# Five large weight matrices of a hybrid decoder block laid out as contiguous 128-column tiles in device memory

## The reference

```python
mod = silu(c) @ w_ada + b_ada            # shift1, scale1, gate1, shift2, scale2, gate2
h    = rmsnorm(x, norm1_g) * (1 + scale1) + shift1
proj = h @ w_in                          # 4096 x 19520: NSA q | NSA k,v | gates(48) | FoX q,k,v | f(16) | merge gates
o_nsa = nsa(...);  o_fox = fox(...)      # two attention mixers, 2048 wide each
g = sigmoid(merge gates)
y = g[..., :D] * (o_nsa @ w_up_nsa) + g[..., D:] * (o_fox @ w_up_fox)
x = x + gate1 * (y @ w_out)              # 4096 x 4096
h2 = rmsnorm(x, norm2_g) * (1 + scale2) + shift2
x = x + gate2 * (square(relu(h2 @ w_ff1)) @ w_ff2)   # 4096 x 16384, 16384 x 4096
```

## Time and profile before

| what | value |
| --- | --- |
| timed runs | 12343.16, 12598.13 (median), 12849.61 us |
| span of the profiled execution, slowest core (5) | 12165.9 us |
| spans of the eight cores | 11995.2 to 12165.9 us |
| PE busy | 9543.8 us, 78% of the span |
| DMA of POOL's queue | 759.01 MB, 66.0% of 16 engines |
| DMA of SP's queue | 329.89 MB, 10.5% of 16 engines |
| chain that ended last | PE 66%, DMA 18%, DVE 6%, ACT 4% |

### The profile page before, as it was taken

How to read it: one execution, slowest core, us unless ns; L and a number is a source line. 1 busy time by engine, 2 the same in 40 slices (tenths; PEclk the granted TensorE clock), 3 DMA queues, 4 the chain that set the end, 5 groups by cost and what they waited for, 6 DMA issues and landing times.

```text
span 12165.9 us, 128077 instructions; the slowest of 8 cores (11995.2 to 12165.9 us)
## 1 busy us (share of the span) xinstructions
PE 9543.8 (78%) x49482; PEld 4455.4 (37%) x49482; DVE 1449.5 (12%) x3744; ACT 1785.7 (15%) x3025; POOL 1166.2 (10%) x830
## 2 busy tenths in 40 slices
PE   1188967888999966666668987598789879987988
PEld 1133332333444434332223433244334334433443
DVE  0101022110000011222322100200000001000000
ACT  0111121112100035322221000200000000000000
POOL 1010000000111100000002300010001001100100
PEclk9887878899999977655557999799889989998999
DMA  9785645677888879533336997799889879988997
GB/s 144 138 90 64 69 92 65 70 71 78 83 93 95 96 123 147 86 56 63 46 60 76 107 108 115 88 68 108 100 75 82 111 93 74 98 106 83 77 107 104
DMA packets 2909954, 1097.08 MB, mean 90 GB/s; under 512 B 2315184, under 2 KB 2897200, under 8 KB 2906288
## 3 DMA queue, kind: packets, MB, share of 16 engines
q0 software_dynamic: 2392608, 759.01, 66.0%
q1 hardware_dynamic: 516752, 329.89, 10.5%
HBM read 1709.32 MB, written 138.41 MB: 152 GB/s over the span
## 4 chain that ended last, share of the span: by engine, by line
PE 66%; DMA 18%; DVE 6%; ACT 4%; issue 4%; SPq 1%; DVEq 0%; another core or an unknown queue 0%; ACTq 0%; POOL 0%; POOLq 0%
PE ps L237 64%; DMA xq_257<-out 5%; DMA ws_55<-w_ada 4%; DMA xq_256<-out 4%; PE ps L240 2%; SPq L266 1%; DMA xp_239<-xc 1%; DVE xr_258 L246 1%; DMA xp_238<-xc 1%; DMA fv_159<-d_fv 1%; DMA ws_56<-w_ff 1%; DVEq L128 0%; ACT hT L243 0%; DVE oaccS L256 0%
## 5 line engine op out<-in xcount | busy, mean ns | idle before, releaser
L237 PE MATMUL ps<-hT,ws_56 128*128 128x512 bf16 x2752 | 643.7, 398 | 18.4 <-DMA ws_56<-w_in 18.0
L237 PE MATMUL ps<-hT,ws_53 128*128 128x512 bf16 (+1 forms) x2688 | 620.0, 394 | 19.2 <-DMA ws_53<-w_in 18.1
L237 PE MATMUL ps<-hT,ws_55 128*128 128x512 bf16 x2688 | 620.4, 394 | 0.6
L237 PE MATMUL ps<-hT,ws_52 128*128 128x512 bf16 (+1 forms) x2688 | 616.1, 392 | 1.5 <-DVE yb_129 L256 0.5
L237 PE MATMUL ps<-hT,ws_54 128*128 128x512 bf16 x2688 | 616.4, 392 | 0.9
L240 PE MATMUL ps<-cf,tn_255 128*128 128x128 f32 x1024 | 180.1, 305 | 501.3 <-DVE xr_258 L246 465.6
L243 ACT ACTIVATE tn_255<-ps,modT 128x512 f32<-128x512 f32 x256 | 175.9, 687 | 2349.1 <-PE ps L240 2315.9
L237 PE MATMUL ps<-oT,ws_56 128*128 128x512 bf16 x2080 | 461.7, 383 | 44.9 <-DMA ws_56<-w_ff 44.9
L237 PE MATMUL ps<-oT,ws_55 128*128 128x512 bf16 x2080 | 461.3, 382 | 28.9 <-DMA ws_55<-w_ff 18.3
L237 PE MATMUL ps<-oT,ws_53 128*128 128x512 bf16 x2016 | 446.4, 382 | 33.2 <-ACT rr_253 L243 25.3
L237 PE MATMUL ps<-oT,ws_52 128*128 128x512 bf16 x2016 | 445.3, 381 | 11.5 <-DMA ws_52<-w_ff 11.5
(11 more groups left out here) (578 smaller groups left out, 10279.4 us busy)
## 6 DMA issues: line engine op xcount, KB each, us to landing
out<-xr_258 SPq DMA_DIRECT2D x256, 256.0 KB, 5.0
ws_56<-w_ff POOLq DMA_DIRECT2D x52, 1024.0 KB, 22.7
ws_52<-w_ff POOLq DMA_DIRECT2D x51, 1024.0 KB, 23.6
ws_53<-w_ff POOLq DMA_DIRECT2D x51, 1024.0 KB, 27.3
ws_54<-w_ff POOLq DMA_DIRECT2D x51, 1024.0 KB, 25.4
ws_55<-w_ff POOLq DMA_DIRECT2D x51, 1024.0 KB, 22.8
ws_56<-w_in POOLq DMA_DIRECT2D x43, 1024.0 KB, 10.7
ws_54<-w_in POOLq DMA_DIRECT2D x42, 1024.0 KB, 10.8
```

Of the source, the lines that this page charges most:

```text
L237: S.emit(PE, lambda e: e.matmul(out_, lhsT, rhs, start=start, stop=stop, skip_group_check=True), reads, writes)
```

## The change

Five matrices (w_in, the two w_up, w_out, w_ff1 and w_ff2) are handed to the kernel in another layout. On the host, `_tiled` cuts a matrix into tiles of 128 columns and stores a tile as 128 partitions, each with all its values of the tile in one run: for 4,096 input rows 32 × 128 values, 16 KB of float32. w_ff2 is cut into its four quarters of 4,096 rows first. The two narrow pieces of w_in, 48 and 16 columns wide, become tensors of their own. In the kernel a source's `W` is now a function from a column to a tile, and the load reads a tile's whole rows. Nothing else is different: w_ada, the slots, the order, the epilogues and the matmuls stay.

```diff
+    def win_tile(col):
+        if col == 5120:
+            return w_g48
+        if col == 11312:
+            return w_f16
+        pad = 0 if col < 5120 else (48 if col < 11312 else 64)
+        return w_in[(col - pad) // 128]
+
+    def tiles_of(W, first=0):
+        return lambda col: W[first + col // 128]
 ...
-                Wv = s_["W"].rearrange("(kc p) n -> p kc n", p=128)
+                Wv = s_["W"](s_["col0"] + c).rearrange("p (kc n) -> p kc n", kc=KC)
                 for kc0 in range(0, KC, 32):
                     nk = min(32, KC - kc0)
                     w = wring.next()
-                    c0 = s_["col0"] + c
-                    S.emit(POOL, (lambda e, w=w, Wv=Wv, kc0=kc0, nk=nk, c0=c0, ncol=ncol:
-                                  e.dma_start(out=w.t[:, 0:nk, 0:ncol], in_=Wv[:, kc0:kc0 + nk, c0:c0 + ncol])),
+                    S.emit(POOL, (lambda e, w=w, Wv=Wv, kc0=kc0, nk=nk, ncol=ncol:
+                                  e.dma_start(out=w.t[:, 0:nk, 0:ncol], in_=Wv[:, kc0:kc0 + nk, :])),
                            [], [w.b], dma=True)
 ...
+def _tiled(W):
+
+    K, N = W.shape
+    return np.ascontiguousarray(W.reshape(K // 128, 128, N // 128, 128).transpose(2, 1, 0, 3)).reshape(
+        N // 128, 128, K)
```

More of the change, by code:

```diff
@@ L194, in build_program @@
     gT_d = din("gT", [128, 64])
-    w_in = din("w_in", [D, DIN])
+    w_in = din("w_in", [152, 128, 4096])
+    w_g48 = din("w_g48", [128, 32 * 48])
+    w_f16 = din("w_f16", [128, 32 * 16])
     bfg_d = din("bfg", [16, 1])
@@ L202, in build_program @@
     w_cv2 = din("w_cv2", [128, 128])
[L203 to L207, removed]
+    w_upa = din("w_upa", [32, 128, 2048])
+    w_upb = din("w_upb", [32, 128, 2048])
+    w_out = din("w_out", [32, 128, 4096])
+    w_ff1 = din("w_ff1", [128, 128, 4096])
+    w_ff2 = din("w_ff2", [128, 128, 4096])
     ropeC_d = din("ropeC", [128, TCTX])
@@ L494, in proj_phase @@
             Rx = Ring(PS[4:8])
-            src = lambda col0: [dict(W=w_in, K=D, col0=col0, inT=hT, kc_off=0)]
+            src = lambda col0: [dict(W=win_tile, K=D, col0=col0, inT=hT, kc_off=0)]
             def epi_raw(dst, g_dst):
@@ L988, in epi_up @@
                 tt(POOL, yT.t[:, ci, t0:t0 + 512], t1.t[:], t2.t[:], ALU.add, [t1.b, t2.b], [yT.b])
-        gemm([dict(W=w_upa, K=2048, col0=0, inT=oT, kc_off=0), dict(W=w_upb, K=2048, col0=0, inT=oT, kc_off=16)],
+        gemm([dict(W=tiles_of(w_upa), K=2048, col0=0, inT=oT, kc_off=0), dict(W=tiles_of(w_upb), K=2048, col0=0, inT=oT, kc_off=16)],
              D, TOWN, [Ring(PS[0:4]), Ring(PS[4:8])], epi_up)
@@ L1018, in epi_res @@
             return f
-        gemm([dict(W=w_out, K=D, col0=0, inT=yT, kc_off=0)], D, TOWN, [Ring(PS[0:4])],
+        gemm([dict(W=tiles_of(w_out), K=D, col0=0, inT=yT, kc_off=0)], D, TOWN, [Ring(PS[0:4])],
              epi_res(64, xc, TOWN, None))
@@ L1043, in build_program @@
         for fc in range(4):
-            specs.append(dict(srcs=[dict(W=w_ff1, K=D, col0=fc * 4096, inT=h2T, kc_off=0)], ncols=4096, T=TOWN,
+            specs.append(dict(srcs=[dict(W=tiles_of(w_ff1), K=D, col0=fc * 4096, inT=h2T, kc_off=0)], ncols=4096, T=TOWN,
                               prings=[Ring(PS[0:4])], epilogue=epi_ff1))
-            specs.append(dict(srcs=[dict(W=w_ff2[fc * 4096:(fc + 1) * 4096, :], K=4096, col0=0, inT=uT, kc_off=0)],
+            specs.append(dict(srcs=[dict(W=tiles_of(w_ff2, 32 * fc), K=4096, col0=0, inT=uT, kc_off=0)],
                               ncols=D, T=TOWN, prings=[Ring(PS[0:4])], epilogue=epi_res(160, out, 0, g_out)))
@@ L1120, in make_in_maps @@
     A_ = lambda a: np.ascontiguousarray(np.asarray(a, dtype=f32))
+    wi = A_(inp["w_in"][0])
     shared = dict(
@@ L1124, in make_in_maps @@
                               np.asarray(inp["norm2_g"][0]).reshape(32, 128).T], axis=1)),
-        w_in=A_(inp["w_in"][0]), bfg=A_(np.asarray(inp["b_forget"][0]).reshape(16, 1)),
+        w_in=np.concatenate([_tiled(wi[:, 0:5120]), _tiled(wi[:, 5168:11312]), _tiled(wi[:, 11328:])]),
+        w_g48=A_(wi[:, 5120:5168].reshape(32, 128, 48).transpose(1, 0, 2).reshape(128, -1)),
+        w_f16=A_(wi[:, 11312:11328].reshape(32, 128, 16).transpose(1, 0, 2).reshape(128, -1)),
+        bfg=A_(np.asarray(inp["b_forget"][0]).reshape(16, 1)),
         qkg=A_(np.stack([np.asarray(inp["nsa_q_norm"][0]), np.asarray(inp["nsa_k_norm"][0]),
@@ L1130, in make_in_maps @@
         w_cv1=A_(inp["w_cmp_v1"][0]), w_cv2=A_(inp["w_cmp_v2"][0]),
-        w_upa=A_(inp["w_up_nsa"][0]), w_upb=A_(inp["w_up_fox"][0]), w_out=A_(inp["w_out"][0]),
-        w_ff1=A_(inp["w_ff1"][0]), w_ff2=A_(inp["w_ff2"][0]),
+        w_upa=_tiled(A_(inp["w_up_nsa"][0])), w_upb=_tiled(A_(inp["w_up_fox"][0])),
+        w_out=_tiled(A_(inp["w_out"][0])), w_ff1=_tiled(A_(inp["w_ff1"][0])),
+        w_ff2=np.concatenate([_tiled(A_(inp["w_ff2"][0][i * 4096:(i + 1) * 4096])) for i in range(4)]),
     )
```

## The result

The changed kernel took 11,361.21 to 11,381.11 us in four timed runs, median 11,372.67. The kernel before took 12,310.88 to 12,849.61 beside it; the ratio is 0.9221 with a 95% interval of 0.9181 to 0.926. Measured again later, with more runs of both on one chip, the ratio was 0.9344 (0.9273 to 0.9414): 11,345.94 to 11,360.31 against 12,093 to 12,245. The prediction was 11,974, with a range that ended at 11,650: the direction was right and the time was far too high.

What follows compares the result with a forecast made beforehand. Weight-load DMA was taken to bound FF1, and residual rounds hitting weight loads FF2. Gains 441 + 96 + 74 + 13 = 624 us off the median 12,598 gave 11,974; likeliest case 11,905 to 12,190, 8-in-10 range 11,650 to 12,320.

Steps and rivals of the forecast that it cites:

- The base: Whole kernel: the timed runs' excess over the profiled span stays, so the gain comes off their median: 12,598 − 624 = 11,974.
- Rival 1: Whole kernel: timed runs have a lower clock than the profile, hiding DMA; 12,489, or 12,317 at two thirds; chance 0.12.
- a load, us of 16 engines: Weight loads: 6.1 us of all engines instead of 14.1, with bounds 5.0 and 7.3.
- FF1, four stages: FF1: DMA falls to 44% and PE alone bounds; 1,774 against 1,870, 96 us gained, at least 48.
- FF2, four stages with what lies behind: FF2: 16.3 us a tile plus 21 us of drain; 2,107 against 2,547.7, 441 us gained (492 to 313).
- w_out: w_out stage: same epilogue with a second x1 buffer; 596.2 to 522, 74 us gained (87 to 42).
- from w_out to the first FF1: Start of the first FF1: PE's 28.6 us wait for the first load shrinks by 13, bounds 5 and 18.
- the best bound: FF2: the load's extra of 8.0 us falls to nothing and PE bounds at 15.9 a tile; 492 us gained.
- the branch that scales it with the load: FF2: the extra shrinks with load length, 8.0 to 3.5 us, so two residual rounds take 17.3 a tile; 313 us gained.
- Rival 2: FF2 and w_out: large weight rows hold up SP's small ones, so these stages keep their time; 12,489; chance 0.05.
- Rival 3: FF1, FF2, w_out: denser matmuls are granted less clock, 3.25 us more on each of 288 tiles; 12,910; chance 0.05.
- Rival 4: Weight loads: the rows are cut up again on the way, nothing changes; 12,598; chance 0.02.

## Why the prediction was wrong, and where it was right

**The base failed.** The step was "I take the difference off the median: 12,598 − 624 = 11,974". It treated what the timed runs have above the profiled span as a constant that the change leaves. The repeated kernel before shows that nothing but 2 us lies around a span and that the excess comes and goes with the clock of a die; the changed kernel's first four runs had none of it, which was in part luck, as three of its seven later ones had it. Taken off the 12,100 of the usual clock, the same 624 give 11,476, 0.9% above the 11,373 measured. The prediction's own 11,542, off the profiled span, was 1.5% above and was set aside; the range's low end, 12,343 − 693 = 11,650, stood on the same base. Rival 1 had the premise, that the timed runs have a lower clock than the profile, and drew from it that 109 to 281 us would be gained; the other consequence, that a run without it starts from 12,100, was not drawn.

**The sum was 95 us short**, on core 5's own stages:

| term | predicted | measured |
| --- | --- | --- |
| a load, us of 16 engines | 6.1 | 6.0 |
| FF1, four stages | 1,774 (−96) | 1,776 (−94) |
| FF2, four stages with what lies behind | 2,107 (−441) | 2,055 (−493) |
| w_out | 522 (−74) | 479 (−118) |
| from w_out to the first FF1 | −13 | 167.7 to 153.3 (−14) |
| sum | −624 | −719 |

12,100 − 719 = 11,381: with both corrections the sum comes out at the measured time, as near as the base is known. On core 5 of the repeated kernel before the same terms (FF1, FF2, w_out, the start) fell by 112, 495, 118 and 11, which is 736, and 12,088.7 − 736 = 11,353, where the changed kernel's core 5 has 11,347.6. In the profile that the prediction read, core 5's span fell by 818, since its first projection had a lower clock (0.81 in the earlier trace rows): its two projections went from 3,686 us to 3,584 (636 to 4,219), which no term spoke of and which is not the change's, as the repeated kernel before has 3,583 too.

**FF2 and w_out** came out at the best bound (15.9 a tile and 21 us of drain, 2,056) and w_out below its own (509). The step that failed is "part of today's lead comes from PE's own wait, which shrinks, so the truth lies between": the extra of a round with a load in it did not go to nothing but from 8.0 to 4.1 (9.7 − 5.6), near the 3.5 of the branch that scales it with the load. But the other round, held at 6.9, became shorter too, so the two make 15.3 in place of 17.3, inside PE's time, and nothing of the extra is seen. The 15.9 was right by another way than the one that led to it. For w_out, 15.9 a tile was too much: that figure, taken for a tile that waits for nothing, holds a wait of about 1 us a tile (the waits of up to 1.3 us above), which the single `tmp` and `x1` buffers of FF2 would explain, and in w_out PE hardly waits (474.13 us busy of 478.60), 15.0 for each of 32 tiles.

**The reason for the cheaper load was wrong, though its size was right.** The prediction put 14.1 to 6.1 on the length of the pieces. Of these 8 us, 2.6 come from the distance between the pieces (14.1 to 11.5 with longer rows) and the rest from longer runs in contiguous tiles (11.4, 7.8, 6.0). All of the time came with the first 2.6, because 11.5 is already below PE's 13.86 and FF2's work below 15.9. The row that spoke against the prediction's cause was among its own: in the second projection the DMA share was 0.84 with PE full, so a load of w_in, in the same 512-byte pieces, cost at most 13.86 × 0.84 = 11.6 us, and it landed in 10.7 us where w_ff's took 25.4. w_in's rows are 78,080 bytes, no power of two.

**Right:** the load of 6 us, FF1 at 444, 301,600 packets, DMA share of 0.43 to 0.46 in FF1, PE's wait for the addition under 100, and w_in and w_up costing nothing. **Rival 2**, large rows that hold up SP's small ones, left a trace only: one of the two residual loads lands in 8.2 us, the other in 4.3, both inside the rounds above. **Rival 3**, denser matmuls at a lower clock, is not seen: FF1 and FF2 stand at 0.99 to 1.00 in the profile after, with every gap in FF1 closed (no execution at a lower mean clock was profiled). **Rival 4** is excluded by the packet count.

## What to carry to other kernels

Before a relayout, compare the cost of one load (DMA share × length of a stretch / loads in it) between matrices that are read in equal pieces: where one costs more, look at the distance of its rows, and try a few unused values at the end of a row first. A cheaper transfer pays only down to what the stage's other bound needs; here that point was 13.86 us in FF1 and 15.9 in FF2, and everything below is spare, while a stage that the DMA engines bind, as the first one here, gains from any cheaper load. Take a predicted difference off a run at the usual clock, not off a median over runs whose clock differs.

## What the runs showed of the hardware that was not expected

Pieces of 512 bytes in rows of 65,536 bytes cost 14.1 us a load of all 16 engines, and 11.5 in rows of 66,048; 512 bytes of padding in a row were worth some 660 us of this kernel (12,021 to 12,059 against 11,376 to 11,380). The Trainium skill, in "DMA: Bandwidth & Descriptors", section "Latency and other measured facts", tells of slow copies from device memory to device memory at row pitches that are large powers of two, from 2 MiB on, for runs of 16 KiB, with nearly the full rate at 512 KiB; it says that 4 KiB more in the pitch restored the rate and 192 bytes did not. The trace agrees in kind: a loss at a round pitch that a longer row takes away. It differs in size: the runs here are of 512 bytes, the rows 64 KB and 16 KB, and 512 bytes more in a row were enough. (A partition's own pieces lie 8 MB and 2 MB apart, within the page's range, and came 64 KB further apart by it; which of the two distances counts, no run here shows.) Why a round distance holds packets up, no run here shows either.

The granted clock of a die differs from execution to execution of one and the same kernel: 0.768 to 0.887 for the changed one, 11,346 to 12,895 us, a spread larger than all that the change brought.
